# A two-layer decoder step on one core: layer 1's first eight input units on the unscaled x, with the scale applied at their banks

## What is computed

```python
def rms_norm(x, g):
    y = x * rsqrt(mean(x * x, axis=-1) + EPS)
    return y * g

def trunk_layer(x, ...):
    h = rms_norm(x, g_mix_pre)
    proj = h @ w_in            # q, k, v, g_ret, ca, cb, ga, gb
    ...
    u = ca * sigmoid(cb)       # then a depthwise convolution over u
    ...
    x = x + rms_norm(merged @ w_o, g_mix_post)
    h2 = rms_norm(x, g_ffn_pre)
    f = (silu(h2 @ w_ffn_gate) * (h2 @ w_ffn_up)) @ w_ffn_down
    return x + rms_norm(f, g_ffn_post), ...
```

## Time and profile before

| | us |
|---|---|
| three runs | 1512.53, 1508.40, 1513.88 |
| median | 1512.53 |
| the profiled execution | 1511.91 |
| its span, first to last instruction | 1509.9 |
| mean granted TensorE clock | 0.997 of 2.4 GHz |

### The profile page before, as it was taken

One profiled execution on the slowest core, in us unless ns is written; L12 is line 12 of the kernel. 1 busy time (PEld: TensorE's weight loads), 2 busy tenths in 40 slices (PEclk: granted clock), 3 DMA queues, 4 the chain that ended last, 5 costly groups with the idle time before them and its releaser, 6 DMA issues.

```text
span 1509.9 us, 25440 instructions
## 1 busy us (share of the span) xinstructions
PE 1475.3 (98%) x9772; PEld 1382.9 (92%) x9772; DVE 1129.1 (75%) x1749; ACT 678.2 (45%) x996; POOL 277.6 (18%) x257
## 2 busy tenths in 40 slices
PE   8999999999999999999999999999999999999997
PEld 8997978888999899999999979788799998999997
DVE  6999999989666567875468897978785766666544
ACT  5343534446454444343343434445454544444433
POOL 5991211120300002556100001122011000000000
PEclk9999999999999999999999999999999999999999
DMA  8447665855545254445445465857644442544443
GB/s 330 140 152 264 237 245 184 321 185 196 166 141 186 89 167 142 150 140 180 155 144 197 161 237 196 306 191 284 226 170 148 140 142 92 170 154 140 157 163 110
DMA packets 64538, 275.46 MB, mean 182 GB/s; under 512 B 7232, under 2 KB 7232, under 8 KB 55232
## 3 DMA queue, kind: packets, MB, share of 16 engines
q1 hardware_dynamic: 52560, 192.17, 38.3%
q0 software_dynamic: 11888, 82.05, 14.5%
HBM read 230.30 MB, written 43.89 MB: 182 GB/s over the span
## 4 chain that ended last, share of the span: by engine, by line
PE 81%; DVE 10%; DMA 4%; ACT 3%; issue 2%; DVEq 0%; ACTq 0%
PE bank L456 24%; PE bank L458 23%; PE bank L457 23%; DVE state L1170 2%; DMA state<-r_in 2%; DVE acc L1139 2%; DVE wlo L1104 2%; DMA rs_out<-state 1%; PE bank L615 1%; PE bank L654 1%; PE bank L476 1%; PE bank L477 1%; PE bank L478 1%; PE bank L596 1%; DVE x L1466 1%
## 5 line engine op out<-in xcount | busy, mean ns | idle before, releaser
L456 PE MATMUL bank<-hhi,whi 128*128 128x320 f32 x2016 | 649.5, 322 | 1.9 <-DVE wlo L1104 1.9
L1104 DVE TENSOR_TENSOR wlo<-wring,whi 128x1024 fp32r<-128x1024 f32 x363 | 483.3, 1335 | 188.5 <-ACT whi L839 159.9
L458 PE MATMUL bank<-hhi,wlo 128*128 128x320 f32 x2016 | 623.8, 309 | 0.0
L457 PE MATMUL bank<-hlo,whi 128*128 128x320 f32 x2016 | 623.3, 309 | 0.0
L456 PEld LDWEIGHTS bank<-hhi,whi 128*128 128x128 f32 x2016 | 379.2, 188 | 22.9 <-issue 21.8
L457 PEld LDWEIGHTS bank<-hlo,whi 128*128 128x128 f32 x2016 | 379.5, 188 | 8.8 <-issue 7.7
L458 PEld LDWEIGHTS bank<-hhi,wlo 128*128 128x128 f32 x2016 | 379.0, 188 | 0.0
L839 ACT ACTIVATE whi<-wring 128x1024 fp32r<-128x1024 f32 x264 | 277.2, 1054 | 212.1 <-PE bank L458 211.6
L1139 DVE SCALAR_TENSOR_TENSOR acc<-up,par,acc 128x256 f32<-128x256 f32 x480 | 210.2, 505 | 0.3
L865 ACT ACTIVATE whi<-wring 128x1024 fp32r<-128x1024 f32 x96 | 101.2, 1054 | 61.6 <-PE bank L458 58.1
L456 PE MATMUL bank<-fhi,whi 128*128 128x320 f32 x352 | 110.6, 314 | 0.0
(11 more groups left out here) (174 smaller groups left out, 1888.3 us busy)
## 6 DMA issues: line engine op xcount, KB each, us to landing
wring<-w SPq DMA_DIRECT2D x364, 512.0 KB, 3.7
state<-r_in POOLq DMA_DIRECT2D x32, 1024.0 KB, 8.4
rs_out<-state POOLq DMA_DIRECT2D x32, 1024.0 KB, 5.0
rp_out<-pst POOLq DMA_DIRECT2D x8, 512.0 KB, 9.3
us<-c_in POOLq DMA_DIRECT2D x2, 1216.0 KB, 5.5
cs_out<-us POOLq DMA_DIRECT2D x2, 1216.0 KB, 8.7
cp_out<-up POOLq DMA_DIRECT2D x2, 1144.0 KB, 5.6
con<-consts POOLq DMA_DIRECT2D x1, 1421.0 KB, 9.6
```

Source lines behind the costliest of these rows:

```text
L456: pe.matmul(bank[g][:, 0:T], whi[j][:, k, :], hi, start=start and k == 0, stop=False)
L457: pe.matmul(bank[g][:, 0:T], whi[j][:, k, :], lo, start=False, stop=False)
L458: mm = pe.matmul(bank[g][:, 0:T], wlo[j][:, k, :], hi, start=False, stop=stop and k == n - 1)
L1104: return dve.tensor_tensor(dst, value, hi.bitcast(F32), ALU.subtract)
```

## The change

Layer 0 is untouched apart from the form of the code. In layer 1:

- A small tile `gpre` holds layer 1's pre-norm gain; POOL loads it at the start of the kernel.
- At the end of layer 0 x is updated in `MIX_GROUPS`. ScalarE writes the upper halves of `x * gpre` to `uhi` and the squares to `sq8`, VectorE writes the lower halves to `ulo` (`ux_low`) and the half sums of the squares (`x_squares`).
- Units 0 to 7 (four pairs, `FREE_PAIRS`) multiply with `uhi` and `ulo`. The mean of squares is formed between the tiles of the first units (`x_both`).
- For these pairs VectorE multiplies the gate's bank by `rstd` into `sig`, ScalarE takes the sigmoid in place, and VectorE multiplies the value's bank by `rstd` into `tmp` before forming `up` and `us`.
- The tiles of `h` for units 8 on are made meanwhile, three, three and two tiles in pairs 0, 1 and 2 (`H_TILES`): values on VectorE, upper halves on ScalarE behind the pair's second weight copy, lower halves on VectorE one pair later. TensorE waits for all eight before unit 8.
- Taps of layer 1 move from pairs 2 and 3 to head 0 (two) and to the last unit of heads 1 to 3 (one each).
- The last layer updates and stores x in the groups of `MIX_GROUPS` too (five stores in place of four), and no longer takes squares or issues clock-keeping matmuls at its end; `keep_clock(20)` at the end of layer 0 becomes `keep_clock(12)`.

```diff
@@ -51,16 +51,18 @@
 AUX_HEAD, AUX_ACT, AUX_DVE = 31, 6, 25
-ROPES, CONVS, POSTS, POSTS0 = 12, TAPS, 18, 10
+ROPES, CONVS, POSTS, POSTS0 = 12, TAPS, 20, 10
 MIX_GROUPS = ((0, 1), (1, 1), (2, 2), (4, 2), (6, 2))
+LOWS = ((), (0,), (1,), (2, 3), (4, 5, 6, 7))
+FREE_PAIRS, H_TILES = 4, ((0, 1, 2), (3, 4, 5), (6, 7))
...
 SAMPLE_OPS = PAST_OPS + NEW_OPS
-CIN_TAPS = ((1, 1, 1, 1, 2, 2), (4, 4, 4, 4, 4, 4))
-FIRST_HEAD_TAPS = ((0, 0, 0, 0, 0, 0, 0, 0, 0, 3, 2, 2), (2, 2, 2, 2, 2, 2, 2, 1, 1, 1, 1, 2))
-HEAD_TAPS = ((5, 0, 3, 0, 3, 1, 5, 3, 3, 0, 0, 2), (7, 0, 3, 0, 4, 0, 5, 4, 3, 0, 0, 2), (6, 0, 3, 0, 3, 0, 3, 2, 2, 0, 0, 0))
+CIN_TAPS = ((1, 1, 1, 1, 2, 2), (1, 2, 4, 4, 4, 4))
+FIRST_HEAD_TAPS = ((0, 0, 0, 0, 0, 0, 0, 0, 0, 3, 2, 2), (2, 2, 2, 2, 2, 2, 2, 1, 1, 2, 1, 3))
+HEAD_TAPS = ((5, 0, 3, 0, 3, 1, 5, 3, 3, 0, 0, 2), (7, 0, 3, 0, 4, 0, 5, 4, 3, 0, 0, 2), (6, 0, 3, 0, 3, 0, 3, 2, 2, 0, 0, 1))
 GB_TAPS = ((6, 0, 3, 3, 3, 1, 4, 0), (5, 0, 3, 3, 2, 1, 3, 0))
@@ -142,6 +144,7 @@
         eps = sb("eps", 1)
+        gpre = sb("gpre", KT)
@@ -161,6 +164,9 @@
         sqz = sb("sqz", KT, T, offset=go_at + KT * T * 4)
+
+        uhi = sb("uhi", KT, T, dtype=F32R, offset=go_at)
+        ulo = sb("ulo", KT, T, dtype=F32R, offset=go_at + KT * T * 4)
@@ -228,6 +234,8 @@
         pad_zeroed = sem("pad_zeroed")
+        gpre_loaded = sem("gpre_loaded")
+        ux_hi, ux_ready, cin_step = sem("ux_hi"), sem("ux_ready"), sem("cin_step")
         h_value, h_hi, h_ready = sem("h_value"), sem("h_hi"), sem("h_ready")
@@ -386,6 +394,7 @@
             pool.dma_start(con[:, :], consts).then_inc(con_loaded, 16)
+            pool.dma_start(gpre[:, :], params[1, :, G_MIXPRE:G_MIXPRE + KT]).then_inc(gpre_loaded, 16)
             for l in range(DEPTH):
@@ -431,11 +440,12 @@
                 pool.dma_start(par[:, :], params[l + 1]).then_inc(par_loaded, 16)
-            for n in range(0, KT, 2):
-
-                pool.wait_ge(post_step, (DEPTH - 1) * POSTS + (POSTS0 + n + 2))
-                pool.dma_start(x_out[:, n:n + 2, :], x[:, n:n + 2, :]).then_inc(x_stored, 16)
-            pool.wait_ge(x_stored, KT // 2 * 16)
+            for i, (k, n) in enumerate(MIX_GROUPS):
+
+                pool.wait_ge(post_step, (DEPTH - 1) * POSTS + (POSTS0 + 2 * i + 2))
+                pool.dma_start(x_out[:, k:k + n, :], x[:, k:k + n, :]).then_inc(x_stored, 16)
+            pool.wait_ge(x_stored, len(MIX_GROUPS) * 16)
+            pool.wait_ge(gpre_loaded, 16)
             pool.wait_ge(par_loaded, (DEPTH + 1) * 16)
@@ -465,17 +475,18 @@
-            h_tile = tile_of(hhi, hlo)
-
-            def first_units(l, q, ready, between=None):
+            h_tile, u_tile = tile_of(hhi, hlo), tile_of(uhi, ulo)
+
+            def first_units(l, q, rhs, ready, between=None):
...
                     for j in range(AHEAD):
-                        pe.matmul(bank[j][:, 0:T], whi[j][:, k, :], hhi[:, k, :], start=(k == 0), stop=False)
-                        pe.matmul(bank[j][:, 0:T], whi[j][:, k, :], hlo[:, k, :], start=False, stop=False)
-                        mm = pe.matmul(bank[j][:, 0:T], wlo[j][:, k, :], hhi[:, k, :], start=False, stop=(k == UB - 1))
+                        hi, lo = rhs(k)
+                        pe.matmul(bank[j][:, 0:T], whi[j][:, k, :], hi, start=(k == 0), stop=False)
+                        pe.matmul(bank[j][:, 0:T], whi[j][:, k, :], lo, start=False, stop=False)
+                        mm = pe.matmul(bank[j][:, 0:T], wlo[j][:, k, :], hi, start=False, stop=(k == UB - 1))
                         if k == UB - 1:
@@ -707,19 +718,44 @@
                     mm.then_inc(stat_done, 1)
-                else:
-                    stat(l, 0, lambda k: sq8[:, k, :], KT, ones_d, lambda k: pe.wait_ge(sq_done, l * SQS + (k + 1))).then_inc(stat_done, 1)
-
-                keep_clock(12)
-                first_units(l, 0, lambda k: h_read(l, k))
-                unit(l, 0, AHEAD, AHEAD, h_tile)
-                with pe.Fori(1, 4) as i:
+                    keep_clock(12)
+
+                def x_half(i):
+
+                    pe.wait_ge(x_halves, l * 2 + (i + 1))
+                    if i == 0:
+                        pe.wait_ge(stat_read, l * STATS)
+                    for k in (4 * i, 4 * i + 1):
+                        mm = pe.matmul(X[:, 0:T], ones_d[:, :], sq8[:, k, :], start=(k == 0), stop=(k == 5))
+                    return mm
+
+                def x_both(k):
+
+                    if k == 5:
+                        x_half(0)
+                    if k == 6:
+                        x_half(1).then_inc(stat_done, 1)
+
+                def cin_round(i, rhs):
                     for j in range(4):
...
                             pe.wait_ge(u_ready, l * 16 + i * 4 + (j - 3))
-                        unit(l, i, j, j, h_tile)
+                        unit(l, i, j, j, rhs)
+
+                if l == 0:
+                    first_units(l, 0, h_tile, lambda k: h_read(l, k))
+                    unit(l, 0, AHEAD, AHEAD, h_tile)
+                    with pe.Fori(1, 4) as i:
+                        cin_round(i, h_tile)
+                else:
+                    first_units(l, 0, u_tile, lambda k: pe.wait_ge(ux_ready, (l - 1) * KT + (k + 1)), between=x_both)
+                    unit(l, 0, AHEAD, AHEAD, u_tile)
+                    cin_round(1, u_tile)
+                    pe.wait_ge(h_ready, l * 16 + KT)
+                    with pe.Fori(2, 4) as i:
+                        cin_round(i, h_tile)
@@ -803,7 +839,7 @@
-                first_units(l, U_GU // RING, lambda k: h_read(l, 8 + k), between=both_halves)
+                first_units(l, U_GU // RING, h_tile, lambda k: h_read(l, 8 + k), between=both_halves)
                 unit(l, U_GU // RING, AHEAD, AHEAD, h_tile)
@@ -823,7 +859,8 @@
                 square_mean(l, SQ_POST2, KT - 1).then_inc(stat_done, 1)
-                keep_clock(20)
+                if l + 1 < DEPTH:
+                    keep_clock(12)
@@ -964,9 +1001,9 @@
-            def halves_of_h(l):
-
-                for k in range(KT):
+            def halves_of_h(l, tiles):
+
+                for k in tiles:
                     act.wait_ge(h_value, l * 8 + (k + 1))
@@ -989,18 +1026,29 @@
             for l in range(DEPTH):
+                if l:
+                    split(l, U_CIN)
                 act.wait_ge(stat_done, l * STATS + 1)
                 rsqrt(l, X[:, 0:T], 0, 0)
-                halves_of_h(l)
+                if l == 0:
+                    halves_of_h(l, range(KT))
                 for n in range(KT):
-                    split(l, U_CIN + 2 * n)
-                    if n >= 4:
-
-                        act.wait_ge(u_ready, l * 16 + (2 * (n - 4) + 2))
-                    gemm(l, U_CIN + 2 * n)
-                    sigmoid(sig[:, n % 4, :], bank[(2 * n) % 4][:, 0:T])
+                    if l == 0 or n:
+                        split(l, U_CIN + 2 * n)
+                    if l and n < FREE_PAIRS:
+
+                        act.wait_ge(cin_step, (l - 1) * (2 * FREE_PAIRS) + (2 * n + 1))
+                        sigmoid(sig[:, n % 4, :], sig[:, n % 4, :])
+                    else:
+                        if n >= 4:
+
+                            act.wait_ge(u_ready, l * 16 + (2 * (n - 4) + 2))
+                        gemm(l, U_CIN + 2 * n)
+                        sigmoid(sig[:, n % 4, :], bank[(2 * n) % 4][:, 0:T])
                     split(l, U_CIN + 2 * n + 1)
+                    if l and n < len(H_TILES):
+                        halves_of_h(l, H_TILES[n])
                 head(l, 0, True)
@@ -1092,9 +1140,14 @@
-                for k in range(KT):
-                    act.wait_ge(post_step, l * POSTS + (POSTS0 + k // 2 * 2 + 2))
-                    act.activation(sq8[:, k, :], x[:, k, :], ACT.Square).then_inc(sq_done, 1)
+                if l + 1 < DEPTH:
+                    act.wait_ge(gpre_loaded, 16)
+                    for i, (k0, n) in enumerate(MIX_GROUPS):
+                        act.wait_ge(post_step, l * POSTS + (POSTS0 + 2 * i + 2))
+                        for k in range(k0, k0 + n):
+                            act.activation(uhi[:, k, :], x[:, k, :], ACT.Copy, scale=gpre[:, k:k + 1]).then_inc(ux_hi, 1)
+                        for k in range(k0, k0 + n):
+                            act.activation(sq8[:, k, :], x[:, k, :], ACT.Square).then_inc(sq_done, 1)
@@ -1114,16 +1167,22 @@
+            def h_value_of(l, k):
+                dve.scalar_tensor_tensor(out=acc[:, k, :], in0=x[:, k, :], scalar=g_(G_MIXPRE + k), in1=rstd[:, :],
+                                         op0=ALU.mult, op1=ALU.mult).then_inc(h_value, 1)
+
+            def h_low_of(l, k):
+                dve.wait_ge(h_hi, l * 16 + (k + 1))
+                lower(hlo[:, k, :], acc[:, k, :], hhi[:, k, :]).then_inc(h_ready, 1)
+
             def normalised(l):
...
                     if k < KT:
-                        dve.scalar_tensor_tensor(out=acc[:, k, :], in0=x[:, k, :], scalar=g_(G_MIXPRE + k), in1=rstd[:, :],
```

(57 more changed lines are left out.)

## The result

The changed kernel takes 1515.07 us in the median of 20 runs (1512.95 to 1517.45), the kernel before 1510.86 in 20 runs of its own (1508.12 to 1514.52). The ratio is 1.0025, with a 95% interval of 1.0018 to 1.0032: 2.7 to 4.8 us slower, 3.8 by the ratio and 4.2 by the medians. The forecast was 1516.8 us, 4.9 us slower; 1515.07 lies 1.7 us under it and inside the range of 1507 to 1520.5. The profiled execution took 1515.34 us, with a span of 1513.4.

What follows compares the result with a forecast made beforehand. The prediction took TensorE, busy for nearly the whole span, to bound the kernel. Chain +3.1, clock +1.5 and tail +0.3 gave +4.9 us on the profiled 1511.91 us, so 1516.8 us, with a range of 1507 to 1520.5 us.

Steps and rivals of the forecast that it cites:

- The earlier start: Border between the layers: layer 1's first product 9.0 us earlier, unit 3 5.48 us earlier, copied from the stage before gate/up.
- The first four pairs: Layer 1's units up to 8: VectorE and ScalarE wait for each other, unit 8 starts 3.1 us later than before.
- rival (b): Layer 1's first pairs: the engines keep up as in gate/up, 5.2 us faster, 1506.7 us; chance 0.13.
- The table load: ScalarE, pair 0: the sigmoid's load follows the root, the next function starts 1.30 us after the load's start.
- The clock: TensorE behind the 5.2 us wait at unit 8: the granted clock falls to 0.50, costing 1.5 us (0 to 3.0).
- The taps and the tail: Heads and end of layer 1: moved taps covered by VectorE's waits, 0; two single-tile groups cost 0.26 us more.
- Rival (c): Layer 1's heads: taps in their last units are not covered, 4.0 us on top, 1520.8 us; chance 0.08.
- Rival (a): Unit 8: the chain binds, but the clock stays up or its fall is harmless, 1515.3 us; chance 0.17.
- The sum: Whole kernel: +3.1 (chain) +1.5 (clock) +0.3 (tail) = +4.9 us, 1516.8 us; chance 0.60.

Runs made afterwards that it cites:

- the one moved copy: The changed kernel with ScalarE's copy of the next unit's weights ahead of the tile copies in pairs 0 to 2; ratio 1.002 to the kernel before.
- the rewritten order: The changed kernel with ScalarE doing both of a pair's weight copies, then the previous pair's tile copies, then the sigmoid; ratio 0.9986 to the kernel before.
- small tiles: The changed kernel with layer 1's normalised tiles made for 8 of their 320 columns only; ratio 1.0001 to the kernel before.
- the rerun: The changed kernel itself timed once more, beside the version with the clock held; 1514.98 us, ratio 1.002 to the kernel before.
- The larger artificial delay: The kernel before with 52 more unread matmuls ahead of layer 1's first product, which started 10.8 us late; ratio 1.0069.
- the small parts alone: The kernel before with only the gain's load, groups of one and two tiles ending both layers, five stores, nothing unread at the very end; ratio 1.0002.
- the taps alone: The kernel before with the changed kernel's tables of taps and nothing else; ratio 1.0001.

## Why the prediction was right, point by point

**The earlier start** was right to within 0.02 us at the first product and at unit 3, because it is a copy of a place that stands in the trace of before.

**The first four pairs** were right in mechanism and size: unit 8 at 43.14 for 42.89, and so 3.3 us of loss for 3.1. Each of the three late units was there, in order. The reason given (ScalarE's weight copy stands behind its wait for the values; VectorE's next weight subtraction stands behind that) is shown by the one moved copy, worth 1.96 us at unit 8, and by the rewritten order, worth 6.7 us there with the same work. Two readings of mine were off. That the tiles are what makes it late, which I took into the experiment with small tiles, is half true: without most of their work 4.5 of the 8.8 us were still there. And the gate/up stage, which rival (b) leaned on, gives no evidence on this, since there the weight copies wait behind nothing.

**The table load** was on the chain for 1.28 us and the next function began 1.29 to 1.30 us after its start, in all three places. The 2.66 us that the Trainium skill gives ("ScalarE: Activation LUTs", "What ACT_TABLE_LOAD costs") are not seen here; a second load delayed unit 8 by 1.27 us.

**The clock** was the term that was mis-sized, at 1.5 us for 2.1: I took the stretch of 3.4 us from the earlier trace rows, and it was 6.8 long, of which TensorE worked 4.5. The Trainium skill ("TensorE: Matmul & The Clock Gate", "Why this matters for your kernels") warns that a pause between bursts of matmuls brings the low clock back. The trace agrees for the wait of 5.3 us; waits of 3.3 us (small tiles) and 1.9 us (rewritten order) brought it as well, for 3.4 us each, and waits of 1.33 and 0.94 us ahead of units 5 and 7 did not.

**The taps and the tail** were right: the taps' 0.5 us in head 0 is given back within the next head, the later heads keep their intervals, and the end is 0.25 us longer (5.90 us from its first to its last update for 5.65). Rival (c), uncovered taps, is excluded. Rival (a), a clock that stays up, did not occur in either profile of the changed kernel. Rival (b), engines that keep up, is not what this kernel did (unit 8 stands at 43.14); the kernel with the new order and six pairs does it, with 5.7 us where 5.2 was worked out.

**The sum** is where something stays open. With the sizes measured in the traces it is 3.3 + 2.1 + 0.3 = 5.7 us, and the ratio says 3.8 (2.7 to 4.8), the rerun 3.0 (1.5 to 4.5). So the forecast's 4.9 was partly luck: its clock term was too small by 0.6, and about 2 us of loss (1 to 3) that the traces show do not arrive. From the first update of `x` at the border to the first at the end of layer 1 the two profiles of the changed kernel take 749.8 and 748.2 us, the one of before 744.6: 5.2 and 3.6 us more, where chain and clock add up to 5.4. The larger artificial delay arrives nearly whole, and the small parts alone change nothing that can be measured (1.2 us faster to 1.8 slower).

The cost of the low clock is the term one would doubt, since holding the clock won 0.9 us, not 2.1. The record does not bear that out. All four profiles of kernels with the wait of 5.3 us have the stretch at its full length of 6.8 us. The mean granted clock of the 20 executions lies between 0.993 and 0.996. At 0.996 some 12 us of the span were at half clock, and the end of the run alone takes 8.6 to 10.3 us of that in these profiles, so by this estimate the stretch was shorter in the two executions that have 0.996; the other 18 leave room for all of it. Where the missing 2 us go stays open.

## What to carry to other kernels

When a wait is added to an engine that also serves another stream, write down what is queued behind it: here a weight copy with all its inputs ready stood behind a wait for another engine's values, and each engine's idle time was the other's wait. A chain across two in-order engines can be costed from durations and starts that are in the trace, before the change is built; the sum of VectorE's work alone (18.5 us against 17.6) would have shown a tenth of the lateness (0.9 of 8.8 us). And when the serial work between two stages is moved beside the next stage, give it the number of steps that its sum asks for: the rewritten order and six pairs in place of four turned 4 us of loss into 6 us of gain; the order alone gave 2 us of gain.

## What the runs showed of the hardware

A pause of TensorE can cost more than itself. With a pause of 5.3 us ahead of unit 8 the granted clock stood at 0.50 for 6.8 us and cost 2.1 us of work; with pauses of 3.3 and 1.9 us there it fell 0.7 and 0.6 us after the work had begun again and stood at 0.50 for 3.4 us; pauses of 1.33 and 0.94 us ahead of units 5 and 7 left it at 1.00, while one of 1.03 us before 220.4 in the trace had been followed by a fall. Unread matmuls in the pause (22, some 5 us) held it at 1.00 in both profiles.

Such stretches also come and go from one execution to the next. In other profiles one of 3.4 us stands near 450 us (the changed kernel's second profile), one of 6.8 us near 341 (the moved weight copy) and one of 6.8 us near 1088 (the taps alone), the last two right behind waits of 1.7 us for a state load. At half speed these cost up to 1.7 and 3.4 us by estimate, so that much of a difference between two single profiles can be due to them.

A switch of ScalarE's function table takes 1.28 us, and the next function starts 1.29 to 1.30 us after the load's start, also when two loads stand one behind the other.
